# Forget-gate running sums as rounded two-part products, and the scaling of pooled modulation units moved from GpSimd to ScalarE

## What is computed

```python
mod = (silu(c) @ ada_w[l] + ada_b[l])          # 6 * 1024 modulation values
h = rmsnorm(x, norm1_g[l]) * (1 + sc1) + sh1
proj = h @ w_in + b_in                         # queries, keys, values, gates
log_f = log_sigmoid(f_logit)                   # 256 rows x 5 heads
F = cumsum(log_f, axis=1)
logits = q @ k.T * scale + F[rows] - F[keys]   # heads C, causal
y = gate_0 * (o_a @ w_a) + gate_1 * (o_b @ w_b) + gate_2 * (o_c @ w_c)
x = x + g1 * (y @ w_out)
x = x + g2 * swiglu(rmsnorm(x, norm2_g[l]) * (1 + sc2) + sh2)
```

## Time and profile before

| | |
|---|---|
| median of 3 runs | 1457.46 us (1456.02, 1457.46, 1462.77) |
| profiled execution, its own time | 1455.73 us |
| its span | 1453.9 us |
| TensorE busy | 1430.9 us, 98% of the span |
| GpSimd busy | 1210.1 us, 83% |
| ScalarE busy | 756.1 us, 52% |
| VectorE busy | 723.1 us, 50% |
| granted TensorE clock, mean | 0.997 of full |

### The profile page before, as it was taken

How to read it: one execution, slowest core, us unless ns; L and a number is a source line. 1 busy time by engine, 2 the same in 40 slices (tenths; PEclk the granted TensorE clock), 3 DMA queues, 4 the chain that set the end, 5 groups by cost and what they waited for, 6 DMA issues and landing times.

```text
span 1453.9 us, 21549 instructions
## 1 busy us (share of the span) xinstructions
PE 1430.9 (98%) x7600; PEld 1199.5 (83%) x7600; DVE 723.1 (50%) x1555; ACT 756.1 (52%) x1274; POOL 1210.1 (83%) x984
## 2 busy tenths in 40 slices
PE   7999999999999999999999999999999999999997
PEld 5898777799988987778888888778888888788886
DVE  7863654766643754745566304454650044655202
ACT  4435775644444445765544445674654346665431
POOL 3899989898978987559898997966999977789994
PEclk9999999999999999999999999999999999999999
DMA  9994547688875986337676565644556756346661
GB/s 361 402 355 159 198 170 223 230 309 310 313 267 166 396 311 213 116 100 230 220 244 202 187 204 170 190 142 144 190 188 201 218 162 187 124 168 203 200 198 52
DMA packets 149415, 313.35 MB, mean 216 GB/s; under 512 B 10918, under 2 KB 31802, under 8 KB 149307
## 3 DMA queue, kind: packets, MB, share of 16 engines
q1 hardware_dynamic: 147552, 310.62, 63.5%
q10 hardware_dynamic: 1756, 1.35, 0.3%
HBM read 310.87 MB, written 1.06 MB: 215 GB/s over the span
## 4 chain that ended last, share of the span: by engine, by line
PE 92%; DVE 4%; ACT 1%; POOL 1%; issue 1%; DMA 1%; SPq 0%; DVEq 0%; ACTq 0%
PE bank L793 58%; PE bank L838 12%; PE bank L839 8%; PE bank L836 5%; PE bank L1001 1%; PE bank L985 1%; POOL lo_units L737 1%; PE bank L874 1%; PE bank L971 1%; DMA x_rows<-in_x 1%; PE bank L1084 1%; PE bank L1017 1%; PE bank L1053 1%; PE bank L1100 1%; PE bank L1043 0%
## 5 line engine op out<-in xcount | busy, mean ns | idle before, releaser
L737 POOL TENSOR_TENSOR lo_units<-raw_units,hi_units 128x512 fp32r<-128x512 f32 (+3 forms) x928 | 1151.4, 1275 | 220.7 <-ACT hi_units L1379 219.5
L1379 ACT ACTIVATE hi_units<-raw_units 128x1024 fp32r<-128x1024 f32 (+1 forms) x470 | 482.6, 1030 | 410.4 <-PE bank L793 239.0
L793 PE MATMUL bank<-hi_units,turned 128*128 128x512 f32 (+3 forms) x1600 | 441.3, 390 | 1.4 <-DVE turned L1914 0.9
L793 PEld LDWEIGHTS bank<-hi_units,turned 128*128 128x128 f32 x1600 | 291.7, 189 | 53.7 <-issue 3.3
L839 PE MATMUL bank<-turned,lo_units 128*128 128x256 f32 x1024 | 287.9, 281 | 0.0
L793 PE MATMUL bank<-hi_units,turned_wide 128*128 128x512 f32 x992 | 274.5, 391 | 0.0
L838 PE MATMUL bank<-turned,hi_units 128*128 128x512 f32 x736 | 258.7, 396 | 0.0
L793 PE MATMUL bank<-lo_units,turned 128*128 128x512 f32 (+3 forms) x800 | 252.6, 383 | 0.8 <-POOL lo_units L737 0.5
L793 PEld LDWEIGHTS bank<-hi_units,turned_wide 128*128 128x128 f32 x992 | 185.3, 188 | 38.6 <-issue 0.5
L839 PEld LDWEIGHTS bank<-turned,lo_units 128*128 128x128 f32 x1024 | 194.3, 190 | 0.2
L793 PEld LDWEIGHTS bank<-lo_units,turned 128*128 128x128 f32 x800 | 149.7, 188 | 30.7 <-POOL lo_units L737 3.7
(11 more groups left out here) (262 smaller groups left out, 1287.9 us busy)
## 6 DMA issues: line engine op xcount, KB each, us to landing
ada_units<-in_ada_w SPq DMA_DIRECT2D x88, 512.0 KB, 7.7
raw_units<-in_w_ffn_tiles SPq DMA_DIRECT2D x72, 512.0 KB, 5.6
raw_units<-in_mlp_w_out SPq DMA_DIRECT2D x64, 512.0 KB, 3.3
raw_units<-in_mlp_w_tiles SPq DMA_DIRECT2D x56, 512.0 KB, 3.3
raw_units<-in_w_in SPq DMA_DIRECT2D x56, 458.0 KB, 9.8
raw_units<-in_w_in SPq DMA_DIRECT2D x48, 512.0 KB, 6.7
raw_units<-in_w_ffn_out SPq DMA_DIRECT2D x44, 512.0 KB, 3.5
raw_units<-in_moba_w_qkv SPq DMA_DIRECT2D x24, 512.0 KB, 3.7
```

What stands on the lines that cost most here:

```text
L737: pool.tensor_tensor(LO[:, s, b, 0:w], RAW[:, u["slot"], b, 0:w], HI_[:, s, b, 0:w].bitcast(F32), ALU.subtract).then_inc(lo_ready.sem, lo_ ...
L793: ins = pe.matmul(BANK[2 * c["pair"] + t][:, 0:w], (A[a] if A is BT else A[:, a])[:, part, t * P:(t + 1) * P], W[:, s, b, 0:w], start=(i = ...
L1379: act.activation(HI_[:, s, 0:n, 0:w], RAW[:, u["slot"], 0:n, 0:w], ACT.Copy)\
```

## The change

1. `forget_products`: the row sums use the rounded format. `log_forget` writes `LF` and its two rounded parts `LFR`, high and low; `tri` is cast once, in place, to the rounded format (its values are 0 and 8). The first row tile's parts move 256 columns each; the second's only the 128 columns that are not zero. The three five-column products stay in fp32.
2. The pooled units: ScalarE scales both halves in place (`scale_pooled`) right after it casts gate units 0, 4, ... 28, and issues the load of the next pooled unit (`load_pooled`) after gate units 2, 6, ... 26, on its own queue. SP keeps the first of the eight loads. GpSimd waits for ScalarE's scaling and only adds.

```diff
...
     ONES = ONES_R[:, :].bitcast(F32)
+    LFR, _ = place("forget_rounded", [P, 2, NT * HC], F32R)
...
     n_early, n_const = cat["inv"][1], cat["dil0"][0]
-    CON, _ = place("constants", [P, n_const])
+    CON, con_at = place("constants", [P, n_const])
+    CON_R, _ = place("constants_rounded", [P, n_const], F32R, at=con_at)
+    TRI_R = CON_R[:, cat["tri"][0] + P:cat["tri"][1]]
+    TRI = TRI_R.bitcast(F32)
...
 
+    pooled = [i for i in ada_ring if i["home"] == "mod"]
     low_order = [(u["l"], u["c"]) for u in ada_ring if u["i"] == 0 and in_two(u["l"], u["c"])]
     low_slot = {chunk_: n % 2 for n, chunk_ in enumerate(low_order)}
 
...
                 sp.dma_start(VEC[:, n % NV, 0:ncols], row.to_broadcast([P, ncols])).then_inc(vec_in[n % NV], 16)
                 continue
             old = item["evicts"]
+            if item["kind"] == "ada" and item["home"] == "mod" and item["turn"]:
+                continue
             if old is not None and old["kind"] == "w":
 
                 sp.wait_ge(lo_ready.sem, lo_ready.at((old["index"], old["n"] - 1)))
...
     @block.gpsimd
     def _(pool):
         first_gate = by_key["gate", 0, 0]["units"][0]["index"]
-        pooled = [i for i in ada_ring if i["home"] == "mod"]
+        sums_left = list(pooled)
 
         def modulation_sum(u):
 
-            pool.wait_ge(ada_in["mod"][0], 16 * (u["turn"] + 1))
+            pool.wait_ge(act_side.sem, act_side.at(("scaled", u["index"])))
             total = MOD[:, u["c"] * CW:(u["c"] + 1) * CW]
             for k in range(UNIT_K):
                 kt = u["i"] * UNIT_K + k
-                part = ada_raw(u)[:, k, :]
-                ins = pool.tensor_scalar(part if kt else total, part, COND[:, kt:kt + 1], None, ALU.mult)
-                if kt:
-                    ins.then_inc(pool_chain.sem, pool_chain.mark(("scaled", u["c"], kt)))
-                    pool.wait_ge(pool_chain.sem, pool_chain.at(("scaled", u["c"], kt)))
-                    ins = pool.tensor_tensor(total, total, part, ALU.add)
+                if kt == 0:
+                    continue
+                ins = pool.tensor_tensor(total, total, ada_raw(u)[:, k, :], ALU.add)
                 if k < UNIT_K - 1:
                     ins.then_inc(pool_chain.sem, pool_chain.mark(("added", u["c"], kt)))
                     pool.wait_ge(pool_chain.sem, pool_chain.at(("added", u["c"], kt)))
...
             for b in range(n):
                 pool.tensor_tensor(LO[:, s, b, 0:w], RAW[:, u["slot"], b, 0:w], HI_[:, s, b, 0:w].bitcast(F32),
                                    ALU.subtract).then_inc(lo_ready.sem, lo_ready.mark((u["index"], b)))
-            if u["index"] >= first_gate and (u["index"] - first_gate) % 4 == 0 and pooled:
-                modulation_sum(pooled.pop(0))
+            if u["index"] >= first_gate and (u["index"] - first_gate) % 4 == 0 and sums_left:
+                modulation_sum(sums_left.pop(0))
 
 
     @block.tensor
...
                     pe.wait_ge(rows.sem, rows.at(("logf", l)))
                     pe.wait_ge(late_const_in, 16)
                     lf = LF.rearrange("p (t h) -> p t h", t=NT)
-                    pe.matmul(BANK[TP][:, 0:HC], con("tri")[:, P:2 * P], lf[:, 0, :], start=True, stop=True)
-                    pe.matmul(BANK[TP][:, HC:2 * HC], con("tri")[:, S:3 * P], lf[:, 0, :], start=True, stop=False)
-                    pe.matmul(BANK[TP][:, HC:2 * HC], con("tri")[:, P:S], lf[:, 1, :], start=False, stop=True)\
+                    pe.matmul(BANK[TP][:, 0:HC], TRI[:, 0:P], lf[:, 0, :], start=True, stop=True)
+                    pe.matmul(BANK[TP][:, HC:2 * HC], TRI[:, P:S], lf[:, 0, :], start=True, stop=False)
+                    pe.matmul(BANK[TP][:, HC:2 * HC], TRI[:, 0:P], lf[:, 1, :], start=False, stop=True)\
                         .then_inc(forget.sem, forget.mark((l, "cols")))
                     return
                 pe.wait_ge(rows.sem, rows.at(("forget cols", l) if c == 1 else ("forget mask", l, c - 2)))
-                pe.matmul(BANK[TP][:, 0:S], LF[:, c - 1:c].to_broadcast([P, P]), con("tri")[:, P:3 * P], start=True, stop=False)
-                pe.matmul(BANK[TP][:, 0:S], LF[:, HC + c - 1:HC + c].to_broadcast([P, P]), con("tri")[:, 0:S], start=False, stop=True)\
-                    .then_inc(forget.sem, forget.mark((l, c - 1)))
+                for t, cols, onto in ((0, slice(0, S), slice(0, S)), (1, slice(0, P), slice(P, S))):
+                    for part in range(2):
+                        ins = pe.matmul(BANK[TP][:, onto], LFR[:, part, t * HC + c - 1:t * HC + c].to_broadcast([P, P]), TRI_R[:, cols],
+                                        start=(t, part) == (0, 0), stop=(t, part) == (1, 1))
+                ins.then_inc(forget.sem, forget.mark((l, c - 1)))
 
             attention(l, heads, PROJ, weave, ONE)
 
...
     def _(act):
         w_units = [i for i in ring if i["kind"] == "w"]
         done = [0]
+        first_gate = by_key["gate", 0, 0]["units"][0]["index"]
+
+        def scale_pooled(u):
+
+            act.wait_ge(ada_in["mod"][0], 16 * (u["turn"] + 1))
+            total = MOD[:, u["c"] * CW:(u["c"] + 1) * CW]
+            for k in range(UNIT_K):
+                kt = u["i"] * UNIT_K + k
+                part = ada_raw(u)[:, k, :]
+                ins = act.activation(part if kt else total, part, ACT.Copy, scale=COND[:, kt:kt + 1])
+            ins.then_inc(act_side.sem, act_side.mark(("scaled", u["index"])))
+
+        def load_pooled(u):
+
+            act.wait_ge(ada_pooled.sem, ada_pooled.at(u["evicts"]["index"]))
+            src = dram["ada_w"][u["l"]].rearrange("(p k) n -> p k n", p=P)[:, u["i"] * UNIT_K:(u["i"] + 1) * UNIT_K, u["c"] * CW:(u["c"] + 1) * CW]
+            act.dma_start(ada_raw(u), src).then_inc(ada_in["mod"][0], 16)
 
         def prep(upto):
 
...
                 act.activation(HI_[:, s, 0:n, 0:w], RAW[:, u["slot"], 0:n, 0:w], ACT.Copy)\
                     .then_inc(hi_ready.sem, hi_ready.mark(u["index"]))
                 done[0] += 1
+                n, part = divmod(u["index"] - first_gate, 4)
+                if part == 0 and 0 <= n < len(pooled):
+                    scale_pooled(pooled[n])
+                if part == 2 and 0 <= n < len(pooled) - 1:
+                    load_pooled(pooled[n + 1])
 
         def bring_exp_table():
 
...
                 after(key)
 
             dve.wait_ge(late_const_in, 16)
+            if l == 0:
+                v.tensor_copy(TRI_R, con("tri")[:, P:3 * P])
             z = PROJ[:, :, FC:FC + HC]
             as2 = lambda a: a.rearrange("p (t h) -> p t h", t=NT)
             link(v.tensor_scalar(as2(ZN), z, -1.0, None, ALU.mult))
...
                 else:
                     dve.wait_ge(act_side.sem, act_side.at(("zl", l)))
                     link(v.tensor_tensor(ZL, ZL, ZD, ALU.subtract))
-                    say(v.scalar_tensor_tensor(LF, ZN, 0.0, ZL, ALU.max, ALU.add), ("logf", l))
+                    link(v.scalar_tensor_tensor(ZN, ZN, 0.0, ZL, ALU.max, ALU.add))
+                    v.tensor_copy(LF, ZN)
+                    link(v.tensor_copy(LFR[:, 0, :], ZN))
+                    say(v.tensor_tensor(LFR[:, 1, :], ZN, LFR[:, 0, :].bitcast(F32), ALU.subtract), ("logf", l))
 
             def mask_of(hd, l=l):
                 if hd["kind"] == "B":
```

## The result

| | before | changed |
|---|---|---|
| median of the runs | 1457.48 us (7 runs, 1456.02 to 1462.77) | 1464.79 us (7 runs, 1463.77 to 1466.29) |
| ratio, 95% interval | | 1.0044 [1.0030, 1.0058] |
| span of the profiled execution | 1453.9 us | 1464.5 us |
| TensorE, GpSimd, ScalarE busy, us | 1430.9, 1210.1, 756.1 | 1432.8, 1184.9, 766.5 |

The change is slower by 6.4 us by the ratio (0.0044 of 1457.5; the two medians of the table lie 7.3 us apart), where the prediction said 1453.5 us and gave 1458.0 as its upper end. The page shows GpSimd's 25 us less, as forecast, and nothing of where the time went: TensorE is still busy for 98%.

A forecast was written before the change was run, and what follows sets the result against it. The prediction took TensorE, busy for 98% of the span, as the bound. Its terms, -4.0 - 0.2 + 1.25 = -2.95 us from 1456.4, gave 1453.5 us, range 1450.0 to 1458.0.

The forecast's parts named there:

- Forget sums: Forget gate's row sums on TensorE: 0.46 us a head instead of 0.86, saving 4.0 us for ten heads.
- All of it reaches the end: Row-sum steps of both layers: TensorE works there without a gap, so its whole 4.0 us saving shortens the time.
- GpSimd's relief behind the attention: Branch products behind layer 0's attention: low parts no longer late once GpSimd loses its scalings, -0.2 us.
- Eighth pair: ScalarE's scalings behind gate unit 28, before the last head's scores: no gap there, +1.25 us all on the path.
- Seven pairs at nothing: ScalarE's scalings behind gate units 0 to 24: they fit its idle gaps, costing nothing.
- The loads at nothing: ScalarE's pooled loads: issues fit its gaps, and the first, out by 110.8 us, lands by 114.8, before its scaling.
- rival 3: Load for gate unit 4 late, stopping ScalarE before a copy TensorE needs: up to 3.3 us, 1456.8 us; chance 0.09.
- Rival 4: Behind gate units 0 to 28 ScalarE's gaps do not hide the pairs: +9.0 us, 1465.4 us; chance 0.07.

The follow-up runs named there:

- e1: The change with forget_rounded placed behind all other buffers, so that every buffer keeps its old address; 1456.48 us, ratio 0.9988 to the kernel before.
- e7: The kernel before with only the shorter rounded sums, forget_rounded behind all other buffers, pooled scalings left on GpSimd; 1456.05 us, ratio 0.9992.
- e8: The kernel before with only the pooled scalings and their loads moved to ScalarE, sums in fp32, no new buffer; 1459.42 us, ratio 1.0011.
- e9: The change with forget_rounded behind all other buffers and ScalarE's second and last scaling pairs one gate unit later; 1454.58 us, ratio 0.9967 to before.
- e6: The kernel before with hi_units and lo_units alone 96 bytes higher, what follows 512 bytes higher; 1465.95 us, ratio 1.0054.
- e10: The change with forget_rounded ahead of every buffer, so that the turned activations move along too; 1460.71 us, ratio 1.0015 to the kernel before.
- e3: The kernel before with 64 unused bytes a partition ahead of raw_units and nothing else; 1460.11 us, ratio 1.0001.
- e5: The kernel before with the raw units alone 96 bytes higher, what follows 512 bytes higher; 1458.77 us, ratio 1.0003.

## Why the prediction was wrong

- **The step that failed** stands ahead of all terms: the sum lists what each engine gains and loses, and takes the price of every other instruction as given by the trace of before. The one line that places `forget_rounded` has no term in it, nor a rival. It moved the time by 8.2 us (change less e1), nearly three times the whole forecast change of -2.95: the untouched products of 512 columns take 6.4 ns more, the loads come at 348 instead of 373 GB/s, and the pooled load is 4.45 us late. The diff shows its size, 2 x 10 words, and its place ahead of `raw_units`.
- **Forget sums, -4.0 us: right.** L1290 takes 0.41 us where the pair had 0.86: 0.24 for the two of 256 columns leaves 0.085 us for one of 128, where I took 0.11. The Trainium skill (TensorE: Matmul & The Clock Gate, section Back-to-back issue gap) has about 81 ns for a 128-column matmul in a stream of loads and matmuls. The 85 ns here, an estimate from these rows, lie nearer to that than to the 110 of my row. The product itself saves 0.45 a head, but the gate unit behind takes 2.81 in place of 2.74, so 0.40 reaches the end, the number forecast. That the two misses cancel, 0.05 too dear a product and 0.07 of a slower neighbour left out, is luck. Five heads give -1.98 in layer 1 (658.35 - 551.87 = 106.48 in e1, against 108.46).
- **"All of it reaches the end": right only with part 2.** With the sums alone GpSimd bounds layer 0 (e7), and 1.3 of the 2.0 us are lost there. I read 117.57 against 117.56 us as freedom for 35 us of GpSimd work; it was freedom up to TensorE's own length, and GpSimd was only 0.7 us below it. So once the sums are shorter, GpSimd's relief is worth 1.3 us beside the -0.2 that I gave it.
- **GpSimd's relief behind the attention, -0.2: right.** 14.13 became 13.95 (e1, e8).
- **Eighth pair, +1.25: right.** 1.22 in e8; the wait 0.27 became 1.49.
- **Seven pairs at nothing: right** where the load comes in time; TensorE's waits in e9 are those of before.
- **The loads at nothing: wrong, as rival 3 had it**, and worse than its 3.3 us. Its step was "at the latest 109.2 + 1.57 = 110.8 us", 4.3 us ahead of TensorE's gate unit 0. In e1 the load goes out at 119.24, 3.9 us ahead of it (123.16), so the lead was sound at unchanged addresses. The load itself took 4.4 us there and 5.1 in e8, not 3.5 to 4.0, and was late by 0.24 and 0.34 us, which TensorE did not feel. In the change it goes out at 112.95, only 1.4 us ahead (114.37): gate unit 0 was cast at 107.17 us, where before it was 103.81, because its weights were late (its cast waited for their load), and GpSimd's low parts and first add (111.63 + 1.30) came behind that. It then took 7.16 us instead of the 3.5 to 4.0, beside loads that were catching up at 387 GB/s (117 to 122 us). Gate unit 4's cast was done at 115.7 (113.45 + 2.24), as forecast at 115.33. TensorE waited 4.65 us, and the slow clock behind it cost 2.6 us more, which no rival had.
- **Rival 4 has the time (1465.4) without its reason.** In layer 0 no step but the first and the last shows a wait of TensorE for ScalarE. That its number lies within 1 us of the measured one is luck.
- **e1 is the forecast put to the test** without the shift: the sum says -2.95 us, e1 measured 0.9988, that is -1.7, with -2.95 inside its interval (-3.8 to +0.4), which holds no change as well. (Taken after the fact, its eight executions at a clock of 0.996 or more average 1455.2 us, the 20 such of before 1457.5: -2.3.)

## What to carry to other kernels

A new buffer is part of a change's price list: list every buffer behind it whose address moves, and ask whether matmul operands keep their distance from each other (here 256 bytes more did no harm, 32, 96 and 128 did, 64 a little), and where DMA destinations go (256 bytes off did no harm, 64 and 96 gave slower loads; 32 and 128 were not tried on the raw units). Place small new buffers last. And an engine that "costs nothing" because two stretches with and without its work are equally long has slack only up to where it stands; when the bounding engine gets shorter, ask how far behind it the next one is.

## What the hardware showed that was not expected

- A rounded product of 512 columns takes 227 ns or 233 ns in unbroken runs (32.68 and 33.60 us for 144), by the distance between its moving and its stationary operand in SBUF alone (e6, e10). With the distance changed by 64 bytes it is 229 ns (e3). Products of 458 columns go slightly the other way: 96 take 19.85 us in e6, 20.00 before.
- With the destinations 96 bytes off their old places the loads of the first 50 us come at 348 GB/s instead of 373, with 64 bytes at 363, with 256 at 373, the DMA share being 0.99 in all. With only the raw units 96 bytes off it is 360 (e5).
- After 4.65 us without work TensorE was granted 0.55 of its clock over the next 6.7 us, so that the wait of 4.65 us cost 7.3. Behind e10's wait of 1.53 us at the same place the gate unit took 2.95 us, as without a wait.
- The scaling of 128 x 512 takes ScalarE 0.71 us (L1384) where GpSimd took 1.57.
